# State-space states with the two directions on the two partition halves

## The reference, cut to what matters

```python
def step(h, u_chunk):                       # direction 0
    bu = einsum('btgs,gps->btgp', u_chunk, b_bar)
    ...                                     # xs[t] = lam_bar * xs[t-1] + bu[t]
    y = einsum('btgp,gsp->btgs', xs, cmat).real
...
yc, yl = _s5_direction(flip(uc, 1), flip(ul, 1), lam, dt, bmat, cmat)   # direction 1
yc, yl = flip(yc, 1), flip(yl, 1)
y_l, y_c = y_l + yl, y_c + yc
```

## Time and profile before

| | us |
|---|---|
| three runs: median (lowest, highest) | 1667.13 (1661.58, 1672.02) |
| the profiled execution, its own time | 1667.57 |
| its span | 1665.8 |
| PE busy, PEld busy | 1583.9, 1039.8 |
| DVE, ACT, POOL busy | 728.0, 371.2, 140.0 |

### The profile page before, as it was taken

The page is one execution under the profiler, slowest core; times in us unless marked ns, Lnnn a source line. Parts: engine busy times, 40 slices in busy tenths (PEclk is TensorE's granted clock), DMA queues, the critical chain, the costliest instruction groups (busy, mean ns, idle before and its releaser), DMA issues.

```text
span 1665.8 us, 23440 instructions
## 1 busy us (share of the span) xinstructions
PE 1583.9 (95%) x9612; PEld 1039.8 (62%) x9612; DVE 728.0 (44%) x1541; ACT 371.2 (22%) x874; POOL 140.0 (8%) x232
## 2 busy tenths in 40 slices
PE   4999989999999998999988999999999989999999
PEld 4455546666655566556777888874445554788843
DVE  5889835545589784872670101012301112233300
ACT  1222333333212223213311000000214431311100
POOL 4013420000023122000010000000000000000000
PEclk8999999999999999999999999999999999999999
DMA  9855760410785457466772444444542123444441
GB/s 314 224 165 190 253 215 1 119 47 1 268 259 181 166 176 254 154 243 235 256 265 78 152 151 152 151 177 151 187 151 101 51 101 101 152 152 151 152 139 63
DMA packets 171186, 270.75 MB, mean 163 GB/s; under 512 B 51021, under 2 KB 84920, under 8 KB 169800
## 3 DMA queue, kind: packets, MB, share of 16 engines
q1 hardware_dynamic: 145840, 201.08, 36.0%
q0 software_dynamic: 16512, 42.49, 8.0%
q10 hardware_dynamic: 8728, 25.69, 4.1%
HBM read 226.16 MB, written 42.99 MB: 162 GB/s over the span
## 4 chain that ended last, share of the span: by engine, by line
PE 80%; issue 13%; DMA 2%; DVE 2%; POOL 1%; ACT 1%; POOLq 0%; DVEq 0%; ACTq 0%
PE bank L434 76%; PE bank L437 4%; DMA memory<-in_w_mod 1%; POOL memory L2360 1%; DMA k_scratch<-memory 0%; DMA memory<-in_s_log_dt 0%; DVE memory L2243 0%; POOL k_scratch L2345 0%; ACT memory L1179 0%; ACT memory L1563 0%; ACT memory L1307 0%; DMA memory<-mc_scratch 0%; DVE memory L1927 0%; DVE memory L1635 0%; DVE memory L1960 0%
## 5 line engine op out<-in xcount | busy, mean ns | idle before, releaser
L434 PE MATMUL bank<-memory 128*128 128x256 f32 (+9 forms) x8848 | 1500.6, 365 | 58.0 <-issue 9.9
L434 PEld LDWEIGHTS bank<-memory 128*128 128x128 f32 (+4 forms) x8848 | 951.2, 161 | 562.1 <-issue 442.8
L437 PEld LDWEIGHTS bank<-memory 128*128 128x128 f32 (+1 forms) x764 | 90.3, 144 | 59.2 <-issue 36.8
L437 PE MATMUL bank<-memory 128*128 128x128 f32 (+1 forms) x764 | 104.4, 281 | 20.0 <-ACT memory L1151 8.8
L2345 POOL DMA_DIRECT2D k_scratch<-memory x128 | 76.2, 630 | 13.3 <-ACT memory L1224 12.9
L2339 POOL DMA_DIRECT2D mc_scratch<-memory x32 | 28.0, 874 | 509.4 <-DVE memory L1845 451.2
L2273 DVE SCALAR_TENSOR_TENSOR memory<-bank,memory 128x255 f32<-128x255 f32 x44 | 21.0, 478 | 104.6 <-ACT memory L1589 104.6
L2122 DVE TENSOR_TENSOR memory<-memory 128x256 f32<-128x256 f32 x56 | 23.3, 417 | 84.0 <-ACT memory L1401 84.0
L2171 DVE TENSOR_SCALAR memory<-bank,memory 128x256 f32<-128x256 f32 x16 | 6.6, 478 | 120.7 <-PE bank L434 120.7
L1960 DVE TENSOR_REDUCE memory<-bank 128x1 f32<-128x512 f32 (+1 forms) x48 | 30.2, 684 | 63.6 <-PE bank L434 63.6
L1307 ACT ACTIVATE memory<-bank,memory 128x512 f32<-128x512 f32 (+1 forms) x64 | 36.3, 579 | 87.2 <-DVE memory L1963 87.2
(11 more groups left out here) (254 smaller groups left out, 962.3 us busy)
## 6 DMA issues: line engine op xcount, KB each, us to landing
memory<-in_s_w_glu SPq DMA_DIRECT2D x16, 2048.0 KB, 9.0
memory<-in_w_mod SPq DMA_DIRECT2D x12, 2048.0 KB, 14.2
memory<-in_w_ffn_up SPq DMA_DIRECT2D x22, 1024.0 KB, 6.5
memory<-in_w_in SPq DMA_DIRECT2D x10, 2048.0 KB, 7.9
mc_scratch<-memory POOLq DMA_DIRECT2D x32, 512.0 KB, 4.6
mb_scratch<-memory ACTq DMA_DIRECT2D x32, 512.0 KB, 3.6
memory<-mb_scratch SPq DMA_DIRECT2D x32, 512.0 KB, 5.6
memory<-mc_scratch POOLq DMA_DIRECT2D x32, 512.0 KB, 5.5
```

Source lines behind the costliest of these rows:

```text
L434: return nc.tensor.matmul(o, l, r, start=start, stop=stop, skip_group_check=free)
L437: return nc.tensor.transpose(o, i, ident[0:n, 0:n])
```

## The change

States carry the direction on the partition halves (0 to 63: direction 0, 64 to 127: direction 1) and par in the free dimension. `additions` gives direction 1 a moving operand with a step of -1 within context and latent. ACT copies a unit with two instructions instead of four. `outputs` contracts all 128 partitions, both directions, in 8 calls instead of 16. The recurrence drops its four copies and, at the end of a quarter, reverses the upper half of `xs_lat` with three copies of 64 partitions x 1024. `mc_load` fetches each unit in two DMAs of 256 KB. The poles are rearranged by four small DMAs on POOL ahead of unit 16 instead of by the DVE copy.

```diff
@@ additions (PE)
-                        dr, ri, ql = n // 4, n // 2 % 2, n % 2
-                        for par in range(2):
+                        ri, par, ql = n // 4, n // 2 % 2, n % 2
+                        for dr in range(2):
                             c = dr * 512 + (ql * 2 + ri) * P + 64 * par
-                            last = mm(b[64 * par:64 * par + 64, n * NC:(n + 1) * NC], mb_in[:, u % 3, c:c + 64], u_(q, par, ql * 8 + g),
-                                      n == 0, n == 7, True)
+                            r = u_(q, par, ql * 8 + g)
+                            if dr:
+                                r = over(r[:, NCL - 1:NCL], (NCL, 2), (-1, NCL))
+                            last = mm(b[64 * dr:64 * dr + 64, n * NC:(n + 1) * NC], mb_in[:, u % 3, c:c + 64], r, n == 0, n == 7, True)
@@ outputs (PE)
-                    for dr in range(2):
-                        for ri in range(2):
-                            for par in range(2):
-                                for ql in range(2):
-                                    m, r = 64 * par + 32 * ql, slice(64 * par, 64 * par + 64)
...
-                                    last = mm(banks[4 + 2 * hq + par][m:m + 32, i * P:(i + 1) * P], st, mc_in[r, u % 3, c:c + P],
-                                              False, i == 3 and dr == 1 and ri == 1, True)
+                    for ri in range(2):
+                        for par in range(2):
+                            for ql in range(2):
+                                m, n, c = 64 * par + 32 * ql, ri * 32 + par * 16 + ql * 8 + g, par * 512 + (ql * 2 + ri) * P
+                                st = over(xs_lat[:, q % 2, n:n + 1], (64, NCL))
+                                last = mm(banks[4 + 2 * hq + par][m:m + 32, i * P:(i + 1) * P], st, mc_in[:, u % 3, c:c + P],
+                                          False, i == 3 and ri == 1, True)
@@ additions (ACT)
-                    for dr in range(2):
...
+                    A(over(xs_ctx[:, g:g + 1], (8, 8), (64, NCL)), over(b[:, 0:1], (64, 8), (1, NCL)), ACT.Copy)
+                    ins = A(over(xs_lat[:, q % 2, 64 + g:65 + g], (8, 8), (64, NCL)), over(b[:, NCL:NCL + 1], (64, 8), (1, NCL)), ACT.Copy)
@@ ahead of unit 16 (DVE)
-            link(V.tensor_copy(lam8_kept, lam8.rearrange("p r n -> p (r n)")))
+            V.tensor_copy(small[0:1, 240:241], small[0:1, 200:201]).then_inc(*S.up("lam8_free"))
@@ ahead of the powers (DVE)
+            dve.wait_ge(*S.at("lam8_in"))
@@ recurrence (DVE)
-                    if b == 0 and q >= 2:
-                        dve.wait_ge(*S.at("yc_mm", 8 * q - 9))
-                    ins = V.tensor_copy(over(xs_back[q % 2]...
...
+                back = slice(64, 128)
+                half = 16 * 64
+                link(V.tensor_copy(over(xs_rev[back, 0:1], (64, 16), (1, 64)), over(lat[back, 31 * 64:31 * 64 + 1], (-64, 16), (1, 64))))
+                link(V.tensor_copy(over(lat[back, half:half + 1], (64, 16), (1, 64)), over(lat[back, 15 * 64:15 * 64 + 1], (-64, 16), (1, 64))))
+                V.tensor_copy(lat[back, 0:half], xs_rev[back, :]).then_inc(*S.up("states", q))
@@ POOL
+            def poles_exchanged():
+                pool.wait_ge(*S.at("lam8_free"))
+                flat = lam8.rearrange("p r n -> p (r n)")
+                for dr in range(2):
+                    for par in range(2):
+                        to = over(lam8_kept[64 * dr:64 * dr + 64, 16 * par:16 * par + 1], (32, 2 * NB), (1, 16))
+                        src = over(flat[64 * par:64 * par + 64, 16 * dr:16 * dr + 1], (32, 2 * NB), (1, 16))
+                        pool.dma_start(to, src).then_inc(*S.up("lam8_in", by=16))
...
-                    pool.dma_start(mc_in[:, u % 3, :].rearrange("p (a n) -> p a n", a=8), mc_dram[u]).then_inc(*S.up("mc_in%d" % (u % 3), u, by=16))
+                    for dr in range(2):
+                        src = dview(mc_dram, u * P * 1024 + dr * 512, (1024, 64), (64 * 1024, 2), (1, 512))
+                        pool.dma_start(mc_in[64 * dr:64 * dr + 64, u % 3, :].rearrange("p (a n) -> p a n", a=2), src).then_inc(*S.up("mc_in%d" % (u % 3), u, by=16))
```

More of the change, by code:

```diff
@@ L276, in build @@
         tt_sb = take(16, P)
-        xs_back = (xs_rev, take(NCL * 32))
         pow8_t = xs_lat.rearrange("p a n -> p (a n)")[:, 0:2048].rearrange("p (a n) -> p a n", a=4)
@@ L2151, in recurrence @@
                     link(tt(to, to, t(1), ALU.add))
-                    if b == 0 and q >= 2:
-                        dve.wait_ge(*S.at("yc_mm", 8 * q - 9))
[L2154 to L2160, removed]
+                back = slice(64, 128)
[3 more added lines that the diff above has]
+                V.tensor_copy(lat[back, 0:half], xs_rev[back, :]).then_inc(*S.up("states", q))
+                dve.wait_ge(*S.at("states", q))
             for q in range(NB):
@@ L2345, in taps_store @@
                     pool.dma_start(to, kt[:, kp % 2, (7 - j) * GS:(7 - j) * GS + P]).then_inc(*S.up("k_out%d" % (kp % 2), kp, by=16))
+            def poles_exchanged():
[6 more added lines that the diff above has]
+                        pool.dma_start(to, src).then_inc(*S.up("lam8_in", by=16))
             for half in range(2):
+                if half:
+                    poles_exchanged()
                 for u in range(16 * half, 16 * half + 16):
```

## The result

The changed kernel takes **1678.96 us** (median of eight runs, 1677.22 to 1686.98), the kernel before 1667.07 in its eight beside them (1661.58 to 1672.02): a ratio of 1.0080 with the 95% interval [1.0062, 1.0097]. It is 11.9 us slower, where 6.5 us less were forecast, and it lies above the range. Differences in us are between medians; a ratio is estimated separately, and the two can differ by a tenth of a per cent. The profiled execution of after took 1686.98 us, the longest of its eight and 8 us above their median, so its trace shows 19 us more than the trace of before, not 12.

The account below looks back on a forecast made before the run. PE, busy 95% of the span, was taken to bound the kernel, so an earlier GLU start is kept. Terms 3.2 + 1.3 + 0 + 0.4 - 0.9 + 2.5 = 6.5 us off gave 1660.6 us, range 1654 to 1667.

Parts of the forecast that it names:

- (b): Outputs of units 8 to 15: 1.3 us kept (0.9 to 3.5), with unit 13 still waiting for its load.
- the tail: States of quarter 3 to the GLU: loads of units 27 and 31 land 0.57 us later each, 1.1 lost.
- The rule cited for the loads: Fixed 2.0 us plus time by bytes: a half load takes 0.6 us less than a whole; sum 1.1 better.
- (a): Outputs of units 0 to 7, in dense PE work: 3.2 us kept (2.4 to 3.5).
- ACT's two copies: Last unit before recurrence(3): two copies take about 0.7 us where four took about 1.05; 0.4 earlier (0 to 0.7).
- recurrence(3) with its copies: Quarter 3's recurrence: four copies dropped, three reversing ones added, 0.9 us longer (0.8 to 2.4).
- states to GLU: Unit 24 to the GLU: 2.5 us won (0.5 to 4.8): units 2.6, unit 27's quicker load 1.0, second issues 1.1 lost.
- rival 1: Additions: reading the moving operand backward at half speed costs 13.8 us, giving 1674.4 us; chance 5%.
- POOL at the start: Four small DMAs ahead of unit 16's store: no cost, with 6 us of cover; 3.6 us delay without it.
- the fourth: Rival: the change does not halve a unit's outputs time, so only costs remain, 1668.7 us; chance 3%.
- The second: Rival: the outputs' whole 14.0 us gain arrives, minus 0.9 plus 1 to 3, giving 1651 to 1654; chance 8%.
- The third: Rival: gain goes into PE waits and a low clock lasting into the first GLU tiles, 1664 to 1668; chance 24%.

Follow-up runs that it names:

- run 1: Kernel before, only each C-matrix load split into two DMAs of 64 neighbouring partitions: 1685.44 us against 1666.43, ratio 1.0103.
- run 2: Kernel before, only each C-matrix load split by columns into two DMAs of all 128 partitions: 1667.53 us, ratio 1.0011.
- run 3: Kernel before, only each C-matrix load split into even and odd partitions, 64 a DMA: 1665.61 us against 1667.19, ratio 0.9998.
- run 6: Changed kernel, halves exchanged by four stores a unit long before, so each C-matrix load is one DMA of 128 partitions: 1657.42 us, ratio 0.9940.
- run 7: As run 6, but direction 1's additions read their moving operand forward (states not the reference's): 1663.18 us, ratio 0.9967.
- run 8: As run 6, but one tiny copy replaces each quarter's three reversing copies (direction 1 stays in scan order): 1658.87 us, ratio 0.9956.
- 9 (on 6): As run 6, with a fourth buffer for loaded C matrices, so loads may be issued a unit earlier: 1657.25 us, ratio 0.9943.
- run 5: Kernel before, its single load kept, with only the change's 8 output calls for 16 (direction 1 not the reference's): 1658.15 us, ratio 0.9953.

## Why the prediction was wrong

**The step that failed** is the price of the split load, in two places. In (b) the text says that a unit's last half is issued 1.2 us later, "though the transfers queue for bandwidth anyway"; in the tail, that each load "now lands with its second DMA, 0.57 behind the first: 1.1 lost". Both count the issues alone, as if half the bytes took half of the engines' time. Measured, the split costs 19.0 us on the kernel before (run 1), while the second issue costs nothing that the runs can tell (runs 2 and 3). The lost time lies less in the tail than in the dense part, where the text saw the least: of the traces' +19.0 us, 11.6 stand between recurrence(0) and recurrence(3), and against run 6 it is 18.9 there and 6.6 from the states to the GLU. No rival had this price; all of them took the DMA share of 0.57 to 1.00 in the earlier trace rows as room or as given, not as something that the shape of a DMA changes.

The rule cited for the loads (the Trainium skill, DMA: Bandwidth & Descriptors, section "Anatomy of one DMA — SWDGE (gpsimd) path": a fixed 2.0 us and the rest by bytes; by it the sum would have been 1.1 better) was not borne out either: 256 KB landed 7.0 us after their issue in the median, 512 KB 5.5. Cut by columns, or into even and odd partitions, they landed after 4.9: the rule's direction holds there, 0.6 us less for half the bytes.

**The gain was sized well.** With the load whole (run 6) the change is worth 9.0 us, by its interval 5 to 15, for a forecast of 6.5. By step (the figures come from single traces; from recurrence(0) to recurrence(3) the four one-load kernels, runs 6, 7, 8 and 9 (on 6), took 152.1, 153.8, 156.2 and 156.1 us for 159.4, and from the states to the GLU 18.5, 19.3, 21.4 and 15.3 for 21.0, so an agreement to a tenth is partly luck):

| | forecast | measured |
|---|---|---|
| (a) + (b), to recurrence(3) | -4.5 | -4.4 (run 5); -7.3 in the one execution of run 6 |
| backward reading | 0 | 0 (227 ns for 227) |
| ACT's two copies | -0.4 | 0 (1.06 us for about 1.05) |
| recurrence(3) with its copies | +0.9 | +0.8 (after and run 6) |
| states to GLU | -2.5 | after +4.1; run 6 -2.5 |
| behind the GLU's start | 0 | after +1.6; run 6 +2.8; runs 2 and 3, with before's time, +2.2 and +1.7 |

A record costs the same with 64 and with 128 contracted rows, as forecast: after loads 48 weights of 128*32 in 1.30 us, 27 ns each, as the earlier trace rows have it (0.86 for 32). Run 6 bears out the sum of the tail but not each part of it: the second issue is absent, and the low clock lasted through the whole tail.

What the prediction had right there is its term of 1.0 us for the load of unit 27, which was to be quicker if issued longer after the GLU's last preload (run 6: 1.5 us). The traces with loads at the full rate line up (us from the preload's issue to the load's; us from the load's issue to unit 27's start, which waits for it):

| run | 8 | 2 | 3 | before | 5 | 6 | 7 |
|---|---|---|---|---|---|---|---|
| behind the preload | 3.49 | 4.11 | 4.81 | 5.30 | 6.49 | 7.57 | 7.65 |
| to unit 27 | 6.90 | 6.53 | 5.57 | 5.24 | 4.19 | 3.70 | 3.79 |

This fits run 8: states that come 2 us earlier leave the preload less time ahead of the load. No run moved the preload by itself. In after it was issued 5.05 us behind the preload and took 8.30.

**Two figures don't come out of the prediction's own rows**, without effect on its sum. PE's wait ahead of unit 24 is given as about 5.5 us: with 1.15 us before, PE 8.0 us earlier and the states 4.0, it comes to 5.15; run 6 shows 3.59. And slower by over 1% would have needed rival 1 at 23.2 us, 1.7 times its price, not more than twice.

**ACT** was mis-sized. The price came from L1364, 0.384 us for 128 x 256, which runs a SiLU and writes in runs of 32 floats. The copies write single floats 64 apart, and the old ones, which did so too, took 0.42 us for half the elements. In after they are slower (instructions of the two lines of after, ns minimum/median/maximum):

```profile
L1392 ACT ACTIVATE memory<-bank x32: 602/624/707, 647.5 to 843.3; 128x256 f32<-128x256 f32 x32
...
L1393 ACT ACTIVATE memory<-bank x32: 632/658/722, 647.9 to 843.7; 128x256 f32<-128x256 f32 x32
```

The last unit's two end 1.06 us after the first starts, and four of the old form took about 1.05. That the stride is the reason is read from the code, not tried alone.

**DVE's copies** came at 0.69 us, as taken from L2100: a negative step and 64 partitions in place of 128 change nothing.

**POOL at the start** was covered: the four exchanges run from 449.58 for 2.76 us, and the store of unit 16 starts at 459.00, again on DVE, with 6.67 us idle before it.

**The rivals.** The first (reversed reading) is refuted by the records of runs 6 and 7, the fourth (no gain from half the records) by run 5. The second (gain kept whole, 14.0) is refuted by run 5's 8.3, whose interval ends at 11.7. The third came true in what it described: PE waits, its clock falls to 0.51 before the GLU, and the GLU begins at 0.66. But it named the gain's own idle time as the cause, and in after the idle time is that of late loads; and runs 2 and 3, which gain and lose nothing, begin the GLU at 0.54 and 0.64 and are 2.2 and 1.7 us longer behind its start. So neither the low clock there nor the 1.6 and 2.8 us of after and run 6 can be put down to the change. That its range (1664 to 1668) was missed as well shows that it lacked the same price.

Of the signs named beforehand, the records came as forecast (512 of 128*32 in place of 1024 of 64*32), while recurrence(3) started 12.5 us later in after, not 4.9 earlier.

**Open** stays what of the 11.6 us is waiting and what the lower clock that follows it (mean record of the additions 246 ns for 228), since no run has the one without the other; and what bounds run 6 next, where a fourth buffer shortened the wait for C matrices by 5.1 us and the time by nothing.

## What to carry to other kernels

Before a DMA is cut in two, look at which partitions each part writes, not at bytes and issues: cut by columns or by interleaved partitions it was free here, cut into partitions 0 to 63 and 64 to 127 it cost 1.0% of the kernel. Where halves of a tile must trade places, do it in a store or load that runs when nothing waits (here four small stores in place of one, long before), and keep the load on the path whole. A DMA share near 1 with a low GB/s beside it is the sign to look for, and its cost can appear at other queues' loads as well (4.5 us for B matrices here). Before a stretch of one trace is compared with one of another, see how much it differs between kernels that do the same there: up to recurrence(0) it was 7 us.

## What was not expected of the hardware

- With all DMA engines busy, windows with loads to 64 or to 32 neighbouring partitions moved 227 to 240 GB/s between the recurrences (328 with whole loads), and 268 to 291 in the tail, where SP's preload runs beside them (367 to 375 with whole, column or even/odd loads). The halves alone moved 216 to 229.
- A load of 512 KB issued 3.5 us behind a preload of 2 MB on another queue took 6.9 us to its user's start, one issued 7.6 us behind it 3.7.
- A reversed moving operand of TensorE cost nothing (227 ns), nor did a negative outer step in a DVE copy (691 ns for 64 x 1024, 695 forward for 128 x 1024).
- An ACT copy of 128 x 256 out of a bank that writes single floats 64 apart took 624 and 658 ns (medians of its two lines), a SiLU of the same size that writes runs of 32 floats 384.
